# A hybrid decoder step on one core: K, Q, V and O weights split ahead into DRAM, and another order of the attention steps

## The reference

```python
h += (gelu(n(h) @ w_in) gated by a spatial mix within chunks of 128) @ w_out     # mixer A
h += swiglu(n(h), w_gate[0], w_up[0], w_down[0])                                 # FFN 0, D_FF = 2816
k, v = n(h) @ w_k, n(h) @ w_v;  q = n(h) @ w_q                                   # 16 heads of 64
z = q k^T / 8 + bias                                                             # causal, k_pos < q_pos
a = exp(log_sigmoid(z) + sum over later keys of log_sigmoid(-z))                 # stick-breaking
h += (a @ v) @ w_o
h += swiglu(n(h), w_gate[1], w_up[1], w_down[1])                                 # FFN 1
y = n(h)
```

## Time and profile before

| | us |
|---|---|
| median of 3 runs | 2922.36 (2918.45 to 2926.47) |
| the profiled execution | 2921.54, its span 2919.5 |
| PE matmul busy | 2763.1 (95%), 16657 instructions |
| DVE, ACT, POOL busy | 1350.9, 755.1, 1205.0 (46%, 26%, 41%) |

### The profile page before, as it was taken

The page is one execution under the profiler, slowest core; times in us unless marked ns, Lnnn a source line. Parts: engine busy times, 40 slices in busy tenths (PEclk is TensorE's granted clock), DMA queues, the critical chain, the costliest instruction groups (busy, mean ns, idle before and its releaser), DMA issues.

```text
span 2919.5 us, 41661 instructions
## 1 busy us (share of the span) xinstructions
PE 2763.1 (95%) x16657; PEld 2637.8 (90%) x16657; DVE 1350.9 (46%) x1237; ACT 755.1 (26%) x1080; POOL 1205.0 (41%) x542
## 2 busy tenths in 40 slices
PE   7999999999999999899999999967999999999997
PEld 6989999999999999788787878756999999999997
DVE  5244543333333337566766766663543333333335
ACT  5122210000000002456665655653110000000003
POOL 4542454334433343344444444443454333433340
PEclk9999999999999999899988989966999999999999
DMA  3111111111111112221221122121121111111111
GB/s 111 51 31 37 44 58 45 51 44 44 44 51 44 44 44 94 61 61 39 64 60 36 53 66 63 32 91 67 43 59 44 46 50 44 44 44 51 44 37 60
DMA packets 219619, 152.91 MB, mean 52 GB/s; under 512 B 9258, under 2 KB 207714, under 8 KB 219426
## 3 DMA queue, kind: packets, MB, share of 16 engines
q1 hardware_dynamic: 200930, 139.63, 15.9%
q10 hardware_dynamic: 18496, 10.49, 1.2%
HBM read 128.86 MB, written 21.22 MB: 51 GB/s over the span
## 4 chain that ended last, share of the span: by engine, by line
PE 83%; DVE 6%; issue 5%; POOL 3%; ACT 2%; DMA 0%; ACTq 0%; SPq 0%; POOLq 0%; DVEq 0%
PE ps L706 48%; PE ps L835 17%; PE aux L963 6%; PE ps L889 2%; PE ps L916 2%; DVE sp_part L1572 2%; PE ps L871 2%; PE ps L901 2%; POOL a_part L644 1%; DVE scratch L1423 1%; PE aux L935 1%; PE aux L1005 1%; DVE sp_part L1570 1%; DVE sp L1559 1%; POOL w_raw L634 1%
## 5 line engine op out<-in xcount | busy, mean ns | idle before, releaser
L564 POOL TENSOR_TENSOR w_hi<-w_raw,ones_col 128x1024 fp32r<-128x1024 f32 x146 | 281.1, 1925 | 997.6 <-PE ps L706 674.2
L571 POOL TENSOR_TENSOR w_lo<-w_raw,w_hi 128x1024 fp32r<-128x1024 f32 x167 | 467.6, 2800 | 13.1
L644 POOL TENSOR_TENSOR a_part<-zb,a_part 128x256 fp32r<-128x256 f32 (+2 forms) x96 | 200.9, 2093 | 466.3 <-ACT zb L1243 466.3
L706 PE MATMUL ps<-near_hi,w_hi 128*128 128x352 f32 x1632 | 356.9, 327 | 17.0 <-DVE near_lo L1410 13.1
L706 PE MATMUL ps<-near_lo,w_hi 128*128 128x352 f32 x1632 | 354.2, 325 | 0.0
L706 PE MATMUL ps<-near_hi,w_lo 128*128 128x352 f32 x1632 | 352.8, 324 | 0.0
L706 PEld LDWEIGHTS ps<-near_hi,w_hi 128*128 128x128 f32 x1632 | 278.8, 190 | 21.1 <-issue 11.5
L706 PE MATMUL ps<-in_hi,w_hi 128*128 128x352 f32 x1320 | 286.6, 325 | 4.8 <-issue 3.9
L1537 DVE TENSOR_TENSOR h<-h,ps 128x1056 f32<-128x1056 f32 x160 | 200.2, 1251 | 187.3 <-PE ps L835 187.3
L706 PE MATMUL ps<-in_lo,w_hi 128*128 128x352 f32 x1320 | 285.3, 324 | 0.0
L706 PE MATMUL ps<-in_hi,w_lo 128*128 128x352 f32 x1320 | 283.9, 323 | 0.0
(11 more groups left out here) (218 smaller groups left out, 4501.2 us busy)
## 6 DMA issues: line engine op xcount, KB each, us to landing
w_raw<-in_w_gate_dram SPq DMA_DIRECT2D x44, 512.0 KB, 3.8
w_raw<-in_w_up_dram SPq DMA_DIRECT2D x44, 512.0 KB, 3.8
w_raw<-in_w_down_dram SPq DMA_DIRECT2D x44, 512.0 KB, 3.6
w_raw<-in_a_w_in_dram SPq DMA_DIRECT2D x16, 512.0 KB, 3.9
k_page<-in_cache_k_dram SPq DMA_DIRECT2D x128, 64.0 KB, 1.9
v_page<-in_cache_v_dram SPq DMA_DIRECT2D x128, 64.0 KB, 1.9
h_kept<-h SPq DMA_DIRECT2D x8, 528.0 KB, 2.7
h<-h_kept SPq DMA_DIRECT2D x8, 528.0 KB, 7.3
```

The source lines that it names most:

```text
L564: gp.tensor_tensor(hi, raw, one, ALU.mult).then_inc(w_hi_done, 1)
L571: gp.tensor_tensor(lo, raw, as32(hi), ALU.subtract).then_inc(w_ready, 1)
L644: gp.tensor_tensor(a_part[:, 1, :, c0:TB], zb[:, s % 3, :, c0:TB], as32(a_part[:, 0, :, c0:TB]), ALU.subtract).then_inc(a_split, 1)
L706: last = mm(out[:, c, 0:CH], w[:, ks], x[:, k, c * CH:c * CH + CH], start=(k == 0 and n == 0), stop=(k == KT - 1 and n == 2))
```

## The change

**Weights.** The slabs of K, Q, V (24) and O (8) are split during FFN 0 and kept in DRAM (`kept_hi`, `kept_lo`; 64 half slabs of 128x512, `JOBS`, with one buffer each `pre_raw`, `pre_hi`, `pre_lo` of 128x512). SP loads a half, POOL splits it (`job`) behind each of its own FFN splits, SP stores both parts. At the end of FFN 0 SP waits for all stores. From then on `slab` loads the two finished parts of a slab, 512 KB each, straight into `w_hi` and `w_lo` (the first two into FFN 0's second slots), and PE waits for that load (`slab_in`) instead of POOL. All splits of K, Q, V and O leave the attention and the O stage. POOL keeps `a_low` and `o_low`.

**Order.** PE's step becomes

```diff
+R_O = 3 * PAIRS
+HALF = D // 2
+JOBS = ([(R_O + n // 2, n % 2) for n in range(12)] + [(n // 2, n % 2) for n in range(2 * R_O)]
+        + [(R_O + n // 2, n % 2) for n in range(12, 2 * KT)])
+NJ = len(JOBS)
+J_KQV = 12
+def kept_at(r):
+    if not isinstance(r, int) or r < R_O:
+        return r + J_KQV // 2
+    return JOBS.index((r, 0)) // 2
...
-X1 = {0: ("c", 0), 1: ("p", 1), 2: ("c", 1), 3: ("c", 2), 4: ("c", 3), 5: ("c", 4), 6: ("p", 3), 7: ("c", 5),
-      8: ("c", 6), 9: ("c", 7), 10: ("c", 8)}
-X2 = {0: ("p", 0), 2: ("k", 0), 3: ("k", 1), 4: ("k", 2), 5: ("p", 2), 9: ("v", 0), 10: ("v", 1), 11: ("v", 2)}
+X1 = {0: ("c", 0), 1: ("p", 1), 2: ("c", 1), 3: ("c", 2), 4: ("c", 3), 5: ("c", 4), 6: ("c", 5), 7: ("c", 6),
+      8: ("c", 7), 10: ("c", 8)}
+X2 = {0: ("p", 0), 2: ("k", 0), 3: ("k", 1), 4: ("k", 2), 5: ("p", 2), 6: ("p", 3), 8: ("v", 0), 9: ("v", 1),
+      11: ("v", 2)}
 X_ORDER = [x[s] for s in range(NS) for x in (X1, X2) if s in x]
 AUX_ORDER = [item for item in X_ORDER if item[0] != "c"]
 NA = len(AUX_ORDER)
 CHUNK_STEP = {s: item[1] for s, item in X1.items() if item[0] == "c"}
 S_START, S_SCORES = 0, {1: (0,), 2: (1,), 6: (2,), 7: (3,)}
-S_CAP, S_LOG, S_SOFT, S_LATER, S_EXP, S_VALUES = 8, 8, 9, 9, 10, 11
+S_CAP, S_LOG, S_SOFT, S_LATER, S_EXP, S_VALUES = 8, 8, 9, 9, 10, (10, 11)
...
+            def store_part(j, i=0):
+                at, half = j // 2 + 6 * i, j % 2
+                sync.wait_ge(pre_ready, j + 12 * i + 1)
+                for kept, part in ((kept_hi, pre_hi), (kept_lo, pre_lo)):
+                    dst = kept[ds(at, 1)].rearrange("o p d -> (o p) d")
+                    sync.dma_start(dst[:, half * HALF:half * HALF + HALF], as32(part[:])).then_inc(pre_out, 16)
+            def load_part(j, i=0):
+                r, half = JOBS[j]
+                src = half_slab(b_w_o[0], r - R_O, half) if r >= R_O else half_slab(kqv[r % 3], r // 3 + 2 * i, half)
+                sync.dma_start(pre_raw[:].rearrange("p (k m) -> p k m", k=KT // 2), src).then_inc(pre_in, 16)
+            for n in range(16):
+                ffn_load(0, n)
+                if n == 4:
+                    sync.wait_ge(sq_added, 3 * KT)
+                    load_part(0)
+                if n > 4:
+                    store_part(n - 5)
+                    load_part(n - 4)
+            with sync.Fori(0, (FG - 3) // 2) as i:
+                for c in range(12):
+                    ffn_load(0, 16 + c, i)
+                    store_part(J_KQV + c - 1, i)
+                    load_part(J_KQV + c, i)
+            for n in range(2):
+                ffn_load(0, 6 * FG - 2 + n)
+                for m in range(2):
+                    store_part(NJ - 5 + 2 * n + m)
+                    load_part(NJ - 4 + 2 * n + m)
+            store_part(NJ - 1)
+            sync.wait_ge(pre_out, 32 * NJ)
+            def slab(r, slot_r, par, used, value):
+                sync.wait_ge(used, value)
+                for dst, kept in zip(slab_slot(slot_r), (kept_hi, kept_lo)):
+                    sync.dma_start(as32(dst), kept[ds(kept_at(r), 1)].rearrange("o p d -> (o p) d"))\
+                        .then_inc(slab_in[par], 16)
...
-            def pair(p, c, k_slab=True, more=True):
-                q = Q_KQV + 3 * (p + 1)
-                par = (Q_KQV + 3 * (c + 1)) % 2
-                if more:
-                    load(q + 2, col_slab(w_v, p + 1), par)
-                    load(q + 3, col_slab(w_k, p + 2) if k_slab else col_slab(b_w_o[0], 0), 1 - par)
+            slab(4, 4, 0, tile_done, T_KQV + 3)
+            def pair(p, c, more=True):
+                r, r_of = 3 * p + 5, 3 * c + 5
                 for rnd in (2, 3):
                     k_pages(p, rnd, aux_at(p, ("p", rnd - 2), more) + 1)
                 if not isinstance(p, int) or p > 0:
...
                     sync.wait_ge(s_out, p)
                     sync.dma_start(o_dram[ds(p - 1, 1)].rearrange("o p r -> (o p) r"), o_t[:]).then_inc(o_kept, 16)
                 if more:
-                    load(q + 4, col_slab(b_w_q[0], p + 2) if k_slab else col_slab(b_w_o[0], 1), par)
+                    slab(r, r_of, r_of % 2, chunk_done, 9 * p + 3)
                     for rnd in (0, 1):
                         k_pages(p + 1, rnd, aux_at(p, ("p", rnd + 2)) + 1)
+                    for n in (1, 2):
+                        slab(r + n, r_of + n, (r_of + n) % 2, chunk_done, 9 * p + 3 + 3 * n)
                     v_pages(p + 1, p + 1)
...
+            for n in range(2, KT):
+                slab(R_O + n, R_O + n, n % 2, tile_done, T_O + n - 1)
...
+            def job(j, i=0):
+                r, at = JOBS[j][0], j + 12 * i
+                first = (JOBS[j][1]) * KT // 2
+                pool.wait_ge(pre_in, 16 * (at + 1))
+                if j > 0:
+                    pool.wait_ge(pre_out, 32 * at)
+                raw, hi, lo = (x[:].rearrange("p (k m) -> p k m", k=KT // 2) for x in (pre_raw, pre_hi, pre_lo))
+                if r >= R_O:
+                    one = ones_col[:, 0:KT // 2].unsqueeze(2).to_broadcast([P, KT // 2, P])
+                    gp.tensor_tensor(hi, raw, one, ALU.mult).then_inc(pre_hi_done, 1)
+                    pool.wait_ge(pre_hi_done, at + 1)
+                else:
+                    g = KT * (G_MIX1 if r % 3 == 1 else G_KV) + first
+                    factor = gains[:, g:g + KT // 2].unsqueeze(2).to_broadcast([P, KT // 2, P])
+                    gp.tensor_tensor(hi, raw, factor, ALU.mult).then_inc(pre_hi_done, 1)
+                    gp.tensor_tensor(raw, raw, factor, ALU.mult).then_inc(pre_scaled, 1)
+                    pool.wait_ge(pre_hi_done, at + 1)
+                    pool.wait_ge(pre_scaled, at - J_KQV + 1)
+                gp.tensor_tensor(lo, raw, as32(hi), ALU.subtract).then_inc(pre_ready, 1)
+            q0 = Q_FFN[0]
+            for n in range(16):
+                if n == 2:
+                    pool.wait_ge(tile_done, T_WOUT + KT)
+                split(q0 + n, 0, 0, n % 2, None, 0, 2 if n < 2 else 4)
+                if n >= 4:
+                    job(n - 4)
+            with pool.Fori(0, (FG - 3) // 2) as i:
+                for c in range(12):
+                    split(q0 + 16 + c, 12, i, c % 2, None, 0, 4)
+                    job(J_KQV + c, i)
             for n in range(2):
...
+                split(q0 + 6 * FG - 2 + n, 0, 0, n % 2, None, 0, 4)
+                for m in range(2):
+                    job(NJ - 4 + 2 * n + m)
+            pool.wait_ge(pre_out, 32 * NJ)
...
+            with pool.Fori(0, PAIRS - 1) as p:
+                for s in range(NS):
+                    a_low(p, s)
+            for s in range(NS):
+                a_low(PAIRS - 1, s)
+                if 2 <= s < PAIRS + 1:
...
+            def sample_values(p, c, half):
+                if half == 0:
+                    pe.wait_ge(s_ad, p + 1)
+                    pe.wait_ge(vp_in, 16 * DB * PAGES * (p + 1))
+                    mm(os_, v_row[0:RS, RT, :], s_a[0:RS, 2, :], start=True, stop=False, skip_group_check=True)
+                for n in range(half * DB, half * DB + DB):
                     b, j = divmod(n, PAGES)
                     at = b * 2 * DL
                     last = mm(os_[:, at:at + 2 * DL], v_page[:, n, :], s_a[:, j, at:at + 2 * DL],
                               start=False, stop=(n == DB * PAGES - 1), skip_group_check=True)
-                last.then_inc(s_pv, 1)
+                if half == 1:
+                    last.then_inc(s_pv, 1)
             def pair(p, c, more=True):
-                for s in range(NS + (0 if more else 3)):
+                for s in range(NS + (0 if more else 2)):
                     if s < NS:
                         scores(p, c, s)
-                    for lag, work in ((3, values), (2, carry)):
-                        at = lagging(p, c, s, lag)
-                        if at is not None:
-                            work(*at)
                     if s in X1 and (more or X1[s][0] == "p"):
                         x_turn(p, c, X1[s], more)
-                    if s == S_VALUES:
-                        sample_values(p, c)
+                    if s == S_VALUES[1]:
+                        sample_values(p, c, 1)
                     at = lagging(p, c, s, 1)
                     if at is not None:
                         take_later(*at)
                     if s in X2 and (more or X2[s][0] == "p"):
                         x_turn(p, c, X2[s], more)
                     sample(p, c, s)
+                    if s == S_VALUES[0]:
+                        sample_values(p, c, 0)
+                    for lag, work in ((2, values), (1, carry)):
+                        at = lagging(p, c, s, lag)
+                        if at is not None:
+                            work(*at)
...
-                for s in range(NS + (0 if more else 3)):
-                    for lag, work in ((0, biased), (2, weights), (0, exp_part)):
+                for s in range(NS + (0 if more else 2)):
```

(40 more changed lines are left out.)

189 lines of the change are left out of this document (72 added, 117 removed).

## The result

The change runs at **2933.3 us** (median, 2931.8 to 2935.3) against 2922.6: 1.0040 times the time before, interval 1.0029 to 1.0052. It is slower by 0.4%, where 2890 was forecast; 2933 lies in the range of 2830 to 2942, but on the other side of the time before. The profiled execution has a span of 2931.0 us against 2919.5.

A forecast was written before the change was run, and what follows sets the result against it. PE was taken as full in FFN 0, losing time to waits and low clock in the attention and its borders. Ordinary pairs -13, back-edge pairs -10, pair 7 -5, border -4.5, FFN 0 +1: -31.5, so 2890 us, range 2830 to 2942.

The forecast's parts named there:

- Step 9's dip: Attention, chunkless step 9: behind 4 us of waiting PE's clock drops, charged 4.5 us a pair.
- The border dip: Pair border, after the sample values: clock drop of 3.3 us taken as gone in ordinary pairs, kept behind a back edge.
- Rival C: Attention: clock dips stay at the border and at step 1, +3.3 or +6.6 us a pair; 2918 us, chance 0.20.
- part (1): Nine POOL weight splits per pair leave the attention, 21 us; little credited, as part of the stall sums.
- (2): FFN 0 takes in 64 half splits on POOL, 20 us a group: +1 us, bounds 0 and +24.
- (3): Slab loads of 1 MB instead of 0.5 MB, about 8 us, issued early enough: cost 0.
- (4): Border to the attention: PE's 4.53 us wait for `s_mask`, behind a Q split on POOL, goes: -4.5 us.
- Full-width steps: Attention: ACT's loop of 8.7 us is even with PE's 8.1 to 8.9; charged 0.5 us a pair.
- rival D: Attention: ACT's loop becomes the bound, 9.9 us a full step against PE's 8.4; 2945 us, chance 0.14.
- The waits in steps 9 and 1: Attention, chunkless steps: PE waits 4.0 us for the sample softplus and 2.6 us for the values' low part.
- The estimate of the exchange: Step 9: exponentials, low part of a, capped copy and sample softplus end 5.3 us after the step's start.
- rival B: Attention: the steps fall into place, waits and dips shrink to some 4 us a pair; 2818 us, chance 0.22.

The follow-up runs named there:

- w_alone: Kernel before with only the change's weights part (kept splits in DRAM, slab loads), all attention orders as before: 2873.8 us, ratio 0.984.

## Why the prediction was wrong

- **The step that failed: what the new order's stalls cost in a pair, the clock above all.** Over pairs 1 to 6 the forecast's mean pair is 98.0 us (four of 96.6, two of 100.9); measured were 105.8. Of the 7.8 us between them the work is 0.3. Idle time was put at 7.4 and came to 9.6: 2.2. The clock was put at 5.6 (4.5, and 3.3 more behind a back edge) and came to 10.8: 5.2. Over six pairs that is the 46 us by which the forecast missed them.
- **Where the clock's term went wrong.** Step 9's dip was charged 4.5 us and cost 3.4 in pair 2. Step 1's was charged nothing, and it cost 5.1 over steps 1 to 3 (0.77, 0.82, 0.83), with a wait of 2.1 in step 1 and one of 1.1 behind it in step 2. The premise, "even pairs have some 2 us there now at full clock", was a misreading: in pair 2 before these are two waits, 0.93 in step 1 and 0.79 in step 2, with 2.4 us of matmuls between them. The border dip is gone in the ordinary pairs, as forecast (0.97 in step 11 of pair 2, 0.98 to 1.00 in step 0 of pairs 1, 2 and 4), and stays behind the back edge, where 3.3 us were charged and 3.1 lost (10.78 us at 0.71). Rival C named the dip at step 1 and had it too small, 3.3 us; 2933.3 lies above its range.
- **Weights, part (1), mis-sized the other way.** "I credit little", since the low part of a stays. Measured: -48 us in w_alone (36 of the 50 us between the spans lie in pairs 1 to 6). I priced what stands in PE's wait (POOL's low part), not what made the two meet. Alone this error would have made the forecast too high; it hid a part of the first one.
- **Parts (2), (3), (4):** FFN 0 is unchanged (PE busy 768.05 of 774, 768.58 before), and no wait of PE is on `slab_in`; zero was right, and +1 within what can be seen. At the border -4.5 was expected; pair 0 starts 3.2 us earlier (1181.2 to 1177.9) and is 3.9 shorter: 7.1. The 4.2 us behind the start of the O stage were not foreseen.
- **Full-width steps:** They take 8.7 to 9.3 us in pair 2 (steps 4 to 7) with at most 0.5 idle, so ACT's loop did not become the bound. Two of them pass the 9 us that the prediction gave as a sign of rival D, and D is still not what happened: but for that 0.5 us PE was at work in them.
- **The waits in steps 9 and 1:** 4.0 and 2.6 were forecast, 3.3 (0.48 and 2.86) and 2.1 measured. The estimate of the exchange, 5.3 us, was good: 1458.61 to 1463.64 is 5.0.
- **Idle time that was missed:** step 2's wait for the staged chunk, 1.9 us a pair, because I placed the eviction by its chunk and not by its place in DVE's queue, although the diff shows `out` moved ahead of it; and 3 us of first scores behind each back edge, where I had 1.
- **Credit given to the wrong half.** The order was credited with the wait of step 6 and its dip, 8.8 us. The weights alone take away 2.7 of the wait and the dip. Against w_alone the order had only 1.6 us to win there, and paid for it in four places (steps 9, 1 and 2, and the back edge).
- **Slips of the working:** pair 0 was priced from 99.2 us and had taken 101.2, which is 2 of its 3.9 us; 1.23 and 2.3 are 3.53, where 3.38 was read; by its own 89 us a pair rival B has 17 and not 14 behind a back edge. None of them changes which case came.
- **The sum:** -31.5 forecast, +11.5 measured. Pairs 1 to 6 were to give -20 (four of -2.6, two of -4.9) and gave +26.2; all else was to give -11 (pair 0, pair 7, border, FFN 0) and gave -14.6. The change is a part that wins 48 us, and on top of it a part that loses 60.

## What to carry to other kernels

Price a change by halves before the sum: a good part can be hidden under a bad one, and here the good one, with the low part of a moved to DVE as well, is the kernel to keep: 2835.5 us, or 2831.0 with the new places of the chunks, both 3.0% less than before. Take length less idle less the clock's loss of a repeated stretch first: it came out nearly constant here (83.5 to 86.2 us in 19 kernels of 93 to 124 us a pair), so that nearly all that these kernels won or lost was idle time and the clock. The clock took 0.6 to 2.3 us for each microsecond of idle time in a pair's mean, so a stall can't be priced by its wait alone. When one engine's queue is reordered, list for each light step every operation that now stands ahead of one that PE waits for.
